# Down projections of a four-layer block computed from seven block products instead of eight, by pairs of token tiles

## The reference, cut to what matters

```
f_lat = squared_relu_mlp(modulate(h_lat, sh_f_l, sc_f_l), ff_w1[i], ff_w2[i])    # square(relu(h @ w1)) @ w2
h_lat = layer_norm(ALPHA * h_lat + g_f_l * f_lat, ln_ff_g[i], ln_ff_b[i])
...
h_lat = h_lat + ga2 * conv_ffn(f_lat, w_ffn_up[i], w_ffn_conv[i], b_ffn_conv[i], w_ffn_down[i])
                                                     # (silu(g) * v) @ w_down
```

## Time and profile before

| | |
|---|---|
| median of 3 runs | 4152.85 us (4149.09, 4152.85, 4154.08) |
| span of the profiled execution, first to last instruction | 4146.1 us |
| the profiled execution's own time | not listed apart from the three runs; its span is 6.75 us under their median |
| busy, share of the span | PE 96%, PEld 60%, DVE 42%, ACT 20%, POOL 7% |
| traffic | 320.56 MB read, 78 GB/s over the span |
| chain that ended last | PE 91%, DVE 4%, ACT 3%, DMA 1% |
| L997, of all PE time | 1014.8 us for the stationary blocks of `BIG` |

### The profile page before, as it was taken

One profiled execution on the slowest core, in us unless ns is written; L12 is line 12 of the kernel. 1 busy time (PEld: TensorE's weight loads), 2 busy tenths in 40 slices (PEclk: granted clock), 3 DMA queues, 4 the chain that ended last, 5 costly groups with the idle time before them and its releaser, 6 DMA issues.

```text
span 4146.1 us, 46361 instructions
## 1 busy us (share of the span) xinstructions
PE 4000.2 (96%) x18592; PEld 2478.5 (60%) x18592; DVE 1744.2 (42%) x3023; ACT 830.9 (20%) x1645; POOL 289.1 (7%) x396
## 2 busy tenths in 40 slices
PE   7999999999999999999999997899999999999999
PEld 6676588744455555448744645645555444758864
DVE  0254533101256556534302015737786015538841
ACT  1266111100122312212102113521100012531000
POOL 1000000000003422400000002200000000000000
PEclk9999999999999999999999999999999999999999
DMA  5255011211122222222222212411111112002222
GB/s 184 92 195 193 21 61 51 82 61 41 34 73 92 72 77 96 103 71 92 92 81 82 71 41 83 164 42 55 58 61 61 56 46 75 21 22 92 82 92 76
DMA packets 201201, 325.66 MB, mean 79 GB/s; under 512 B 4274, under 2 KB 90632, under 8 KB 200864
## 3 DMA queue, kind: packets, MB, share of 16 engines
q1 hardware_dynamic: 195136, 302.00, 21.4%
q0 software_dynamic: 5856, 20.73, 1.6%
HBM read 320.56 MB, written 2.16 MB: 78 GB/s over the span
## 4 chain that ended last, share of the span: by engine, by line
PE 91%; DVE 4%; ACT 3%; issue 1%; DMA 1%; POOL 0%; DVEq 0%; ACTq 0%; POOLq 0%
PE PS L997 27%; PE PS L1037 25%; PE PS L970 3%; PE PS L1565 3%; PE PS L948 3%; PE PS L1091 3%; PE PS L1579 3%; PE PS L907 2%; PE PS L821 2%; PE PS L1566 1%; PE PS L1726 1%; PE PS L1736 1%; PE PS L1209 1%; PE PS L1178 1%; PE PS L950 1%; PE PS L1418 1%
## 5 line engine op out<-in xcount | busy, mean ns | idle before, releaser
L997 PE MATMUL PS<-RING,BIG 128*128 128x512 f32 x2352 | 1014.8, 592 | 2.9 <-DVEq L1798 1.6
L997 PEld LDWEIGHTS PS<-RING,BIG 128*128 128x128 f32 x2352 | 444.7, 190 | 554.0 <-issue 549.1
L1037 PE MATMUL PS<-UT,RING 128*128 128x256 f32 (+1 forms) x2432 | 639.2, 410 | 10.4 <-ACT BIG L2668 9.1
L1037 PEld LDWEIGHTS PS<-UT,RING 128*128 128x128 f32 x2432 | 461.0, 190 | 151.0 <-issue 14.2
L1037 PE MATMUL PS<-BIG,RING 128*128 128x256 f32 (+1 forms) x1824 | 487.7, 410 | 0.8 <-DVE BIG L2526 0.5
L1884 DVE TENSOR_TENSOR RES_TMP<-PS,GATE 128x512 f32<-128x512 f32 x80 | 55.3, 692 | 1019.4 <-PE PS L997 949.9
L1037 PEld LDWEIGHTS PS<-BIG,RING 128*128 128x128 f32 x1824 | 345.9, 190 | 106.5 <-DVEq L1818 1.5
L2651 ACT ACTIVATE UT<-PS,COL 128x128 f32<-128x128 f32 x328 | 119.0, 467 | 130.1 <-PE PS L885 128.1
L997 PE MATMUL PS<-RING,UT 128*128 128x512 f32 x320 | 139.2, 593 | 2.0 <-issue 1.2
L1565 PE MATMUL PS<-UT,RING 128*128 128x512 f32 x256 | 132.2, 598 | 3.8 <-issue 3.1
L948 PE MATMUL PS<-UT,RING 128*128 128x512 f32 x256 | 127.7, 594 | 1.0 <-ACT BIG L2863 1.0
(11 more groups left out here) (413 smaller groups left out, 4757.0 us busy)
## 6 DMA issues: line engine op xcount, KB each, us to landing
RING<-w_mod_dram SPq DMA_DIRECT2D x48, 2048.0 KB, 8.2
RING<-w_ffn_up_dram SPq DMA_DIRECT2D x44, 1024.0 KB, 5.1
RING<-ff_w_dram SPq DMA_DIRECT2D x32, 1024.0 KB, 5.5
RING<-ff_w_dram SPq DMA_DIRECT2D x16, 2048.0 KB, 7.9
RING<-ssm_w_in_dram SPq DMA_DIRECT2D x8, 2048.0 KB, 8.1
RING<-w_ffn_down_dram SPq DMA_DIRECT2D x8, 1536.0 KB, 6.6
RING<-w_ffn_down_dram SPq DMA_DIRECT2D x8, 1280.0 KB, 5.9
RING<-ssm_w_out_dram SPq DMA_DIRECT2D x4, 2048.0 KB, 8.0
```

What stands on the lines that cost most here:

```text
L997: m = mm(bank(t), inp[:, kk, t * 128:(t + 1) * 128], w[:, k, :], start=kk == 0, stop=kk == kn - 1)
L1037: m = mm(bank(bank_, n), a[:, k, :], b[:, k, :], start=k == 0, stop=k == 3)
```

## The change

The down projections leave `both_halves` for a function of their own, `paired_down`, on PE, VectorE, ScalarE and SP.

Two token tiles of a pair and two blocks of 128 hidden channels make a 2x2 arrangement a11, a12, a21, a22 (the second index is the channel block), and the 256 weight rows by 1024 columns make b11 to b22. One such step is a slot. PE does seven products in a slot, each of a 128x128 stationary block with 512 moving columns, and each of the seven adds up over all slots of the pair in a bank of its own. Four of the products need sums of token blocks (s1 to s4) and four need sums of weight blocks (t1 to t4). A pair has 16 slots in layers 0 and 1 and 11 in layers 2 and 3; there are 3, 2, 3 and 2 pairs, so 48, 32, 33 and 22 slots.

The weights of a slot are one transfer of 1024 KB into columns 0 to 2047 of a ring slot; columns 2048 to 4095 hold the four weight sums. Every weight row is loaded once for each pair.

VectorE forms all the sums, for slot i+1 while PE works on slot i: four operations on 128x128 and four on 128x512. Between these two groups stand the pieces of work on the pair before (residual, normalisation, scaling), spread by the table in `parts`. At the end of a pair VectorE combines the seven banks in seven steps (`take`), of which PE's next pair waits for one for each bank; ScalarE copies the first product (`first_taken`).

The token tiles of a pair are transposed in halves of four (`turn_half`, into bank 7) after single slots of the next pair; in layer 1 the halves of the context tiles 4 and 5 come first, after slots 1 to 4 of the second pair. The tiles of the last pair (4 and 5, from layer 1 to 2 tiles 2 and 3) are transposed in the next mixer. The next mixer's first products wait for `outputs_begun` and `outputs_taken`, the latter for all seven takes of the last pair. Some buffers of the mixers of layers 2 and 3 get other places.

```diff
-            for name, n in [("out", 4 if L == 1 else 2), ("up", PAIRS[L]), ("down", 8)]:
+            token_pairs = (2 if L in (1, 3) else 3)
+            for name, n in [("out", 4 if L == 1 else 2), ("up", PAIRS[L]), ("down", token_pairs * PAIRS[L] // (1 if L < 2 else 2))]:
...
+            def down(L, w):
...
+                first, n = down_slots_before(L), down_slots(L)
+                for i in range(n):
+                    if i >= 2:
+                        sp.wait_ge(S("down_sums_ready"), down_weights_summed(L, i - 2))
+                    s = i % down_steps(L)
+                    load(RING[:, state["t"] % 2, 0:2048].rearrange("p (k n) -> p k n", k=2), wv[:, 2 * s:2 * s + 2, :])
+                state["slots"] = [first + n - 1, first + n]
...
+            def paired_down(L):
...
+                place_in_takes = {"P2": 1, "P3": 4, "P7": 5, "P5": 6, "P6": 2, "P4": 7}
...
+                    hooks[0, 5] = partial(bias_columns_in_time, N)
+                    hooks[0, 12 if L < 2 else 8] = partial(gate_rows_in_time, N)
+                    if L == 1:
+                        hooks.update({(1, 1 + 2 * i + h): partial(turn_half, N, 4 + i, h) for i in range(2) for h in range(2)})
+                    at = {0: 8, 1: 11, 2: 7}[L]
+                    hooks.update({(q, at + 2 * i + h): partial(turn_half, N, 2 * q - 2 + i, h) for q in range(1, pairs_) for i in range(2) for h in range(2)})
...
+                        weights(t)
+                        pe.wait_ge(S("down_sums_ready"), down_tokens_summed(L, i))
+                        done(product("P1", a11, b11))
+                        done(product("P2", a12, b21))
+                        used(product("P3", s4, b22))
+                        pe.wait_ge(S("down_sums_ready"), down_weights_summed(L, i))
+                        done(product("P7", s3, t3))
+                        done(product("P5", s1, t1))
+                        done(product("P6", s2, t2))
+                        product("P4", a22, t4).then_inc(S("down_slots_done"), 1)
+                        if (q, s) in hooks:
+                            hooks[q, s]()
...
+            def sums_of_down_tokens(L, i):
...
+                if i >= 2:
+                    dve.wait_ge(S("down_slots_done"), first + i - 1)
...
+                step.go(V.tensor_tensor(s3, a11, a21, ALU.subtract))
+                step(V.tensor_tensor(s1, a21, a22, ALU.add))
+                step(V.tensor_tensor(s2, s1, a11, ALU.subtract))
+                V.tensor_tensor(s4, a12, s2, ALU.subtract).then_inc(S("down_sums_ready"), 1)
...
+                def combined(q, early):
...
+                    dve.wait_ge(S("down_first_taken"), g + 1)
+                    dve.wait_ge(S("down_products_done"), 5 * g + 2)
+                    take(V.tensor_tensor(y1, y2, b("P2"), ALU.add))
+                    early()
+                    dve.wait_ge(S("down_products_done"), 5 * g + 5)
+                    take(V.tensor_tensor(y2, y2, b("P6"), ALU.add))
+                    take(V.tensor_tensor(y4, y2, b("P5"), ALU.add))
+                    dve.wait_ge(wused, T0[L, "down"] + (q + 1) * steps)
+                    take(V.tensor_tensor(y4, y4, b("P3"), ALU.add))
+                    take(V.tensor_tensor(y3, y2, b("P7"), ALU.add))
+                    take(V.tensor_tensor(y2, y3, b("P5"), ALU.add))
+                    dve.wait_ge(S("down_slots_done"), first + (q + 1) * steps)
+                    take(V.tensor_tensor(y3, y3, b("P4"), ALU.add))
...
+                    if L == 1:
+                        return {2: [partial(added, q, 0, 1)], 3: [partial(added, q, 1, 0)], 4: [partial(norm, L, "f", a)],
+                                5: [partial(added, q, 1, 1)], 6: [partial(rms_input, N, "m", a)], 7: [partial(norm, L, "f", b)],
+                                9: [partial(rms_input, N, "m", b)]}
...
+                for i in range(n):
...
+                    if i + 1 < n:
+                        sums_of_down_tokens(L, i + 1)
+                    for part in work.get((q, s), ()):
+                        part()
+                    if i + 1 < n:
+                        sums_of_down_weights(L, i + 1)
+                    if s == steps - 1:
+                        combined(q, partial(added, q, 0, 0))
...
                     if p + 1 < PAIRS[L]:
                         sums_of_weights(L, p + 1)
                         post("sums_ready")
+                    else:
+                        sums_of_down_tokens(L, 0)
+                        sums_of_down_weights(L, 0)
...
+                first_taken(0)
...
+                if L == 1:
+                    for t in (4, 5):
+                        turned_half(N, t, 0)
+                        turned_half(N, t, 1)
+                for q in range(pairs_):
...
+                    prepared(a, b)
...
+                            if q < pairs_ - 1:
+                                turned_half(N, t, 0)
+                                turned_half(N, t, 1)
...
+                    if q < pairs_ - 1:
+                        first_taken(q + 1)
```

More of the change, by code:

```diff
@@ L897, in half_freed, with early_tile @@
                     pe.wait_ge(f.free, taken[f] + t + 1)
-            def early_tile(L, which, t, f, old, early, first, rest, hooks):
+            def early_tile(L, which, t, f, freed, early, first, rest, hooks):
                 w = ring(weights(t))
@@ L1767, in _ @@
                 paired_up(L, old)
[L1768 to L1784 removed]
+                paired_down(L)
         @block.vector
@@ L2640, in gate_rows, with turned_half @@
                 post("gate_rows_ready")
+            def turned_half(L, t, half):
+                f = flow(L, "tokens_turned", 1)
+                offer(f)
+                p = int(t >= TL)
+                ready(f)
+                for k in range(4 * half, 4 * half + 4):
+                    step.go(A(UT[:, k, t * 128:(t + 1) * 128], bank(7, 128, k % 4 * 128), ACT.Identity, scale=COL[:, 1, k, p:p + 1], bias=COL[:, 0, k, p:p + 1]))
+                step.settle()
+                post_free(f)
             def turned_tokens(L, which, t, b=6, between=None):
```

405 lines of the change are left out of this document (266 added, 139 removed).

## The result

The changed kernel takes 4101.9 us (median of four runs, 4099.31 to 4106.54), the kernel before 4153.47 (median of four, 4149.09 to 4154.3). The ratio is 0.9884, its 95% interval 0.987 to 0.9898: 1.2% faster, 51.6 us. The forecast was 65.4 us less than before, 4087.5, with a range of 4068 to 4116. The profiled execution took 4101.04 us and has a span of 4099.2; the span of before was 4146.1. On spans the gain is 46.9 us against 65.4, so 18.5 us are missing, and this text looks for them.

What follows compares the result with a forecast made beforehand. PE was taken as the bound, a stage costing what its matmuls cost. -116.1 - 2.8 + 34.6 + 18.9 = -65.4 us on the 4146.1 us span gave 4080.7; plus 6.75 for the median, 4087.5 us, range 4068 to 4116.

Steps and rivals of the forecast that it cites:

- Pace: Down projections: 135 products fewer at an unchanged 0.86 us each, -116.1 us; a slot of seven takes 6.02 us.
- changes of pair: First slot of a new pair: P3 waits for VectorE's fourth take; 2.3 us three times, 1.6 twice, 10.1 us.
- the root: Layer 1: ScalarE's root behind four half tiles delays normalisation and slot 5's weight sums; 5.3 us, and 0.6 next slot.
- the starts of layers 2 and 3: After the first slot, PE waits because takes and last convolutions precede the second slot's sums; 5.9 and 4.3 us.
- the second change in layer 2: Layer 2's second change of pair: a half tile right ahead delays ScalarE's copy of the first product; 5.2 us.
- the gate rows: PE waits for ScalarE's copy of the gate rows, 0.8 us in three layers: 2.4 us.
- 1 to 2: Boundary from layer 1's last product into layer 2: T + 48.7 against 44.1 us before, costing 4.6 us.
- 0 to 1: Boundary from layer 0's last product to layer 1's first on 2048 KB of weights: T + 34.3, costing 7.0 us.
- 2 to 3: Boundary from layer 2's last product (T) into layer 3: 45.9 against 45.1 us, takes not waited for, costing 0.8 us.
- More waits: Rival, chance 0.19: down projections lag more through slower 1024 KB loads or 971 ns sums; 4102 to 4135 us.
- VectorE becomes the bound: Rival, chance 0.06: at 1.6 us per 128x512 sum VectorE bounds the slots, over 4330 us; threshold about 1.0 us a sum.
- Fewer waits: Rival, chance 0.08: parts of the 34.6 us of waits inside the stages don't occur; 4055 to 4074 us.

Runs made afterwards that it cites:

- those with more sums: Two kernels: the changed kernel with one or two more VectorE operations on 128x512 in every down-projection slot; 4119.87 us and 4152.27 us.
- the kernel with the earlier root: Changed kernel, but in layer 1 ScalarE takes the first token tile's root ahead of the halves of tile 5; 4097.05 us.

## Why the prediction was right, and where its sum was off

Direction, mechanism and range were right: fewer products at an unchanged pace, VectorE and the loads hidden, single waits at named places. On spans, in us:

| term | forecast | measured |
|---|---|---|
| 135 products fewer | -116.1 | -116.1 |
| waits inside the stages | +34.6 | +30.4 |
| half clock inside the stages | none | +8.5 |
| boundaries and end | +18.9 | +26.4 |
| start gaps, and the work between the stages | -2.8 | +0.4 |
| not attributed | none | +3.4 |
| sum | -65.4 | -46.9 |

- *Pace.* "Form and engine stay the same, so I take the pace of the earlier trace rows." In undisturbed slots right, 6.01 us for 6.02. **This is the step that failed:** The earlier trace rows are the pace of an engine that never waits, and I kept it for the matmuls behind fifteen waits. Half clock costs 8.5 us in the stages (2.7 + 2.3 + 1.7 + 1.8), 3.0 in L1726 (6.53 for 3.5) and 2.7 in L1068 (30.41 for 27.73), 14.2 us together, against the 18.5 that are missing. One us more lies in L1743: behind its wait of 5.61 half clock costs 2.5 us, and in the kernel before, behind 2.34, it cost 1.5 (see above). That row was in the earlier trace rows, and I read only its start. The Trainium skill, TensorE: Matmul & The Clock Gate, section HAM oscillation — how this bites in real kernels, describes an array that waits for transfers, falls back to half its clock and starts the next block there, and counts that loss beside the wait. By that rule, the runs agree: waits for VectorE and ScalarE, in the place of transfers, are followed by 1.7 to 3.0 us of loss. It would have been a term of the sum.
- *Waits inside.* The changes of pair cost 1.8, 1.8, 1.9, 1.0 and 1.0 us, 7.6 for 10.1; the root 5.2 and nothing in the next slot, for 5.9; the starts of layers 2 and 3 5.95 and 4.24, for 5.9 and 4.3; the second change in layer 2 4.75 for 5.2; the gate rows 1.4 for 2.4; lag of parts in layer 0 1.3 for 0.8.
- *Boundaries.* 1 to 2 cost 4.4 (forecast 4.6) and the end 6.5 (6.5). 0 to 1 cost 10.3 for 7.0, through L1726's clock. 2 to 3 cost 5.1 for 0.8: **the second step that failed** is "the takes end at 9.5 and are not waited for: 45.9". The matmuls do end there, 46.2 us behind T. But I stopped at their end and did not follow ScalarE, which has its chain of 4 us a tile behind the copies of the last token tile, and now only 32 of PE's instructions to hide them in place of 48. The queries' wait rose from 0.9 to 5.0 us, nearly all of the 4.3 that were off.
- *Not attributed.* Of the 3.4 us, 1.3 are transposes that stood behind the last product before and stand ahead of it now: a tile in layer 1 (0.87) and half a tile in layer 2. Each wait also costs more than its idle figure, which counts from the end of an instruction of 0.59 us where the step is 0.43, and the first instruction behind it is 0.10 longer (the eight at 2124.16 take 3.70 for 3.60): 0.26 us, 3.9 for fifteen waits, of which some 0.5 is in the half clock already. Against that, two waits inside the stages of before, 0.96 in layer 1 and 1.06 in layer 2, are gone with their edges, 2.5 us. About 1.2 us stay open.
- *From span to time.* I added 6.75 us, the distance of the old span from its median. The profiled executions of the changed kernel and of all the experiments lie 1.8 us above their spans; the old profile was of a quick execution. That error was to my favour: without it I would have said 4082.5.
- *The rivals.* "More waits" gave 4102 to 4135, and the result lies at its edge, but for none of its reasons: 1024 KB land in 5.0 us and not 8, 128x512 sums take 692 ns and not 971. No execution here had GpSimd at work beside the sums, so the contention stays untried. "VectorE becomes the bound" had its threshold right, and the margin is 0.33 us a sum, though part of what used it up is half clock, which its division did not contain. (Its cost at 1.6 us a sum is too low by its own terms: four such sums and 1.15 are 7.55 us a slot, and 135 times 1.53 is 207, not 185. Nothing hangs on it. In the root's wait 8.2 - 3.0 is 5.2, not 5.3.) "Fewer waits" took the root and the convolutions as given by the program; both could be moved.

## What to carry to other kernels

When a wait is put into a stage that was bound by PE, price it twice: its length, and half clock behind it, here 1.7 to 2.7 us for each wait of 4 us or more. Behind shorter ones, down to 1.9, it came in some executions and not in others: the two of 2.40 and 2.35 in layer 2 had it in the changed kernel and not in those with more sums. The converse is worth as much: edits that remove such waits by order alone (a root ahead of copies, rows that are needed late moved behind sums that are needed now) gave 37 us of span here, beside the 47 of the change itself, for no work saved. And follow a boundary to the first product that waits for nothing from the stage before, not to the end of the matmuls that it feeds.

## What the runs showed of the hardware

- In the down projections, PE went on at a granted clock of half behind every wait of 4.2 us or more, in every trace. From 1.9 to 3.2 us both were seen: at 1.91 us 5.40 us for eight instructions, at 1.94 3.70; in the boundary behind layer 0, at 3.04 us, 6.53 and 6.49 us against 3.72 for the same sixteen. Behind a wait shorter than that, with no other just ahead of it, none was seen in the down projections. Extra matmuls in the wait kept the clock at 1.00.
- The spread between executions of one kernel goes with the clock: the changed kernel's spans are 4097.5 to 4101.0 at a mean of 0.985 and 4104.8 at 0.984, those of the kernel with the earlier root 4094.3 at 0.987 and 4100.4 at 0.985.
- Three and a half times the traffic of before (170 GB/s against 49 in layer 0's stage) did not slow a 1024 KB transfer: 5.0 us, 5.5 before.
